# Three additions per state tile moved from Pool to DVE in the interleaved stage of a four-layer model

## The chip, the core and the metric

The kernel runs on one core of a Trainium2 chip. Its engines are PE (TensorE, matrix products), DVE (VectorE) and ACT (ScalarE), which work on tiles elementwise, Pool (GpSimd), which here rounds and splits weights and does some additions, and SP, which issues most of the transfers. The metric is the device time of one execution in microseconds, and the median of several executions is compared. PSUM, into which PE writes its products, is used here as eight banks of 128 x 512 fp32.

## The reference

Two models of two layers each follow one another on one sequence of 512 tokens and width 1024. The change touches only the second model, where each layer first mixes tokens in three ways, side by side: a state-space mixer, a gated spatial unit and a differential attention.

```python
def s5_mixer(u, a_re, a_im, log_dt, b_re, b_im, c_re, c_im, d_skip, w_glu, b_glu):
    ...
    bu = jnp.einsum("bsgh,gph->bsgp", uf.astype(jnp.complex64), b_bar)
    ...
    _, states = lax.associative_scan(combine, (a_seq, bu), axis=1)
    c_mat = lax.complex(c_re.astype(jnp.float32), c_im.astype(jnp.float32))
    y = jnp.real(jnp.einsum("bsgp,ghp->bsgh", states, c_mat))
    y = y + d_skip.astype(jnp.float32).reshape(SSM_GROUPS, SSM_GROUP) * uf
    y = jax.nn.gelu(y.reshape(bsz, seq, SSM_WIDTH))
    y = y * jax.nn.sigmoid(y @ w_glu.astype(jnp.float32) + b_glu.astype(jnp.float32))
    return y.astype(u.dtype)

def diff_attention(q, k, v, ...):
    ...
    def block(args):
        ...
        p = jax.nn.softmax(s, axis=-1)
        w = (p[:, :, 0] - lam * p[:, :, 1]).astype(v.dtype)
        return jnp.einsum("bhqk,bkhe->bqhe", w, v)
```

There are 16 groups of 64 complex states, that is 1024 states, or 8 tiles of 128 states by 512 positions. The rest of the reference (the first model, the projections and the feed-forward parts) is not touched.

## The kernel before

Every engine has its own program, written out by hand in the order in which it is to run; between them stand semaphores. There is no scheduler. A PSUM bank is named by a key such as ("yp", l, i). PE calls `claim(key)`: keys get the banks 0 to 7 in turn, and PE waits there until the key that had the bank eight claims earlier has been drained. `fill` reports that the bank is written, and the reader's `wait_filled` and `drain` answer to them.

The interleaved stage is run once for each of two layers (l = 0 and 1), from 1984 to 2080 us and from 2708 to 2804 us. It has 8 state tiles, i = 0 to 7, and 32 attention steps, most of them three to a state tile. For one state tile the work is:

- PE, `state_in(i)`: three products into three banks, keys ("bu", l, i, m) (L1123).
- DVE, `turn_in(i)`: three multiplications of these banks with tables of cosines and sums, which write turned[0], turned[1], turned[2] (L2256). This turns the complex input so that the recurrence becomes real.
- Pool: turned[1] = turned[0] + turned[1] and turned[2] = turned[0] - turned[2] (L1833, L1834).
- DVE, `scan(i)`: two scans along the 512 positions, which write z_re and z_im (L2266, L2268).
- Pool: z_sum = z_re + z_im (L1830).
- DVE, `turn_out(i)`: three multiplications that write out_parts (L2277, L2278, L2280).
- PE, `state_out(i)`: three products of out_parts, added up in one bank, key ("yp", l, i) (L1131).
- DVE, `add_y(l, i)`: adds that bank to yg and drains it (L2229 for i = 0 and 4, L2234 otherwise).

One attention step has scores on PE (L717), bias and row maximum on DVE (L1967), the exponential on ACT (L1340), a transposition on PE (L727), its copy on ACT (L1352), the product with v on PE (L739) and its scaling on DVE (L1984 or L1986, with L1976 and L1978 on two columns).

PE's order in tile i is `state_in(i + 1)`, `state_out(i - 1)`, then three attention steps. In tile 1 the gated spatial unit (L1113) stands between the first two. That makes 13 claims for a tile in the steady part, 3 + 1 + 9: ("yp", l, i - 1) is the fourth, and the claim eight places behind it is that of the transposition L727 in the third attention step of the same tile. So this transposition waits until `add_y(l, i - 1)` has drained its bank.

DVE's order in tile i is `scan(i)`, `turn_in(i + 1)`, one attention step, `turn_out(i)`, `add_y(l, i - 1)`, two attention steps. Pool does nothing else in this stage. z_re, z_im, z_sum and turned are single tiles in xnT, not doubled.

The lines of DVE's loop:

```python
scan(i)
if i < 7:
    turn_in(i + 1)
...
a0 = S5_STEPS * i - 3
attention(f"a2_{l}", a0, a0 + 1)
turn_out(i)
if i:
    add_y(l, i - 1)
attention(f"a2_{l}", a0 + 1, a0 + S5_STEPS)
```

Of the kernel before, what the change touches and what calls it, by code (L numbers as in the profile page):

```python
# [11 lines left out]
ALU = mybir.AluOpType  # L12
# [120 lines left out]
def build(nc, A, out, upto=99):  # L133
    ctx = ExitStack()
    with ctx:
# [123 lines left out]
        z_re, z_im, z_sum = (xnT[:, i, :] for i in range(3))  # L259
        turned = [xnT[:, 3 + i, :] for i in range(3)]  # L260
# [71 lines left out]
        def S(name):  # L332
            if name not in made:
                made[name] = ctx.enter_context(nc.semaphore(name))
            return made[name]
# [24 lines left out]
        def wait_filled(eng, key):  # L360
            eng.wait_ge(*filled_sem(key))
            return bank(key)
# [4 lines left out]
        def wait_drained(eng, key):  # L367
            eng.wait_ge(drained_sem(key), number[key] // BANKS + 1)
# [1231 lines left out]
        def _(pool):  # L1600
# [208 lines left out]
            for l in range(L2):  # L1809

                pool.dma_start(wn, A["gmlp_w_s_2"][l].rearrange("h i j -> i h j")).then_inc(S("gmlp_in"), 16)
                pool.dma_start(vgain, A["gmlp_v_g_2"][l:l + 1, :].broadcast_to([P, 256])).then_inc(S("gmlp_in"), 16)
                for i, name in enumerate(("lambda_q1_2", "lambda_k1_2", "lambda_q2_2", "lambda_k2_2")):
                    pool.dma_start(lamrow[:, i, :], A[name][l:l + 1, :].broadcast_to([P, 64])).then_inc(S("gmlp_in"), 16)
                pool.dma_start(subg, A["subln_g_2"][l:l + 1, :].broadcast_to([P, P])).then_inc(S("gmlp_in"), 16)
                pool.wait_ge(S("gmlp_in"), 16 * 7 * (l + 1))
                pool.memset(wn[0:64, :, 64:128], 0.0).then_inc(S("wn_ready"), 1)
                if l == 0:
                    wait_filled(pool, ("oh", NE - 1, 1))
                split(f"in{l}")  # L1820
                split(f"qk{l}", 2)
                rotary(groups2(l), f"g2_{l}", lambda i, l=l: split(f"qk{l}", 2))

                for i in range(-1, 8):
                    n = 8 * l + i
                    if i >= 0:
                        pool.wait_ge(S("scan_done"), n + 1)
                        if n:
                            pool.wait_ge(S("out_parts_ready"), n)
                        pool.tensor_tensor(z_sum, z_re, z_im, ALU.add).then_inc(S("z_sum_ready"), 1)  # L1830
                    if i < 7:
                        wait_drained(pool, ("bu", l, i + 1, 0))
                        pool.tensor_tensor(turned[1], turned[0], turned[1], ALU.add).then_inc(S("bu_turned"), 1)  # L1833
                        pool.tensor_tensor(turned[2], turned[0], turned[2], ALU.subtract).then_inc(S("bu_turned"), 1)  # L1834

                wait_filled(pool, ("mt", f"m2_{l}", NT - 1, 1))
                pool.wait_ge(S("y_copied"), 2 * (l + 1))
                split(f"out2_{l}")
                if upto <= 6 + 2 * l:
                    return  # L1840
                split(f"ff{l}")
                if upto <= 7 + 2 * l:
                    return
# [3 lines left out]
        def _(dve):  # L1847
# [107 lines left out]
            def attention(stage, first=-3, end=None):  # L1955
                base, todo = steps[stage]
                for i in range(first, len(todo) if end is None else end):
                    if i + 3 < len(todo):

                        u, t = todo[i + 3]  # L1960
                        j = base + i + 3
                        n = keys_of(u, t)
                        if i + 3 >= 3:
                            dve.wait_ge(S("probs_ready"), j - 2)
                        key = ("S", j)
                        ps = wait_filled(dve, key)
                        drain(dve.tensor_tensor_reduce(out=s_buf[:, j % 3, 0:n], in0=ps[:, 0:n], in1=bias_of(u, t),  # L1967
                                                       scale=1.0, scalar=3e38, op0=ALU.add, op1=ALU.min,
                                                       accum_out=nmx[:, j % 8:j % 8 + 1]), key)
                    if i >= 0:  # L1970
                        u, t = todo[i]
                        j = base + i
                        if i % 2 == 0:
                            dve.wait_ge(S("probs_ready"), j + 2)
                            pair_cf, gates = coef[:, j % 8:j % 8 + 2], gates_of(u, t)
                            link(dve.reciprocal(pair_cf, psumsum[:, j % 8:j % 8 + 2]))  # L1976
                            if gates is not None:
                                link(dve.tensor_tensor(pair_cf, pair_cf, gates, ALU.mult))  # L1978
                        cf = coef[:, j % 8:j % 8 + 1]
                        key = ("O", j)  # L1980
                        ps = wait_filled(dve, key)[:, u["at"]:u["at"] + u["w"]]
                        dst = u["dst"](t)
                        if u["first"]:
                            drain(dve.tensor_scalar(dst, ps, cf, None, ALU.mult), key)  # L1984
                        else:
                            drain(dve.scalar_tensor_tensor(out=dst, in0=ps, scalar=cf, in1=dst,  # L1986
                                                           op0=ALU.mult, op1=ALU.add), key)
# [248 lines left out]
            for l in range(L2):  # L2236
# [10 lines left out]
                def turn_in(i):  # L2247
# [5 lines left out]
                    for part, m, tab in ((0, 2, 0), (1, 1, 1), (2, 0, 2)):  # L2253
                        key = ("bu", l, i, m)
                        ps = wait_filled(dve, key)
                        drain(dve.tensor_tensor(turned[part], ps[:, :], tabs[:, tab, :], ALU.mult), key)  # L2256

                def scan(i):

                    n = 8 * l + i  # L2260
                    rb = s5("r")[:, n:n + 1].broadcast_to([P, T])
                    if n:
                        dve.wait_ge(S("out_parts_ready"), n)
                        dve.wait_ge(S("z_sum_ready"), n)
                    dve.wait_ge(S("bu_turned"), 2 * n + 1)
                    dve.tensor_tensor_scan(z_re, rb, turned[1], 0.0, ALU.mult, ALU.add)  # L2266
                    dve.wait_ge(S("bu_turned"), 2 * n + 2)
                    dve.tensor_tensor_scan(z_im, rb, turned[2], 0.0, ALU.mult, ALU.add).then_inc(S("scan_done"), 1)  # L2268

                def turn_out(i):  # L2270

                    n = 8 * l + i
                    tabs = s5_tabs[i % S5_BUFS]
                    dve.wait_ge(S("scan_done"), n + 1)
                    if i:
                        wait_filled(dve, ("yp", l, i - 1))
                    dve.tensor_tensor(out_parts[1], z_re, tabs[:, 1, :], ALU.mult)  # L2277
                    dve.tensor_tensor(out_parts[2], z_im, tabs[:, 2, :], ALU.mult)  # L2278
                    dve.wait_ge(S("z_sum_ready"), n + 1)
                    dve.tensor_tensor(out_parts[0], z_sum, tabs[:, 0, :], ALU.mult).then_inc(S("out_parts_ready"), 1)  # L2280
# [8 lines left out]
                for t in range(NT):  # L2289
                    dve.scalar_tensor_tensor(out=vn[:, t, :], in0=ugv[:, t, 256:512], scalar=s5("rstd")[:, t:t + 1],  # L2290
                                             in1=vgain, op0=ALU.mult, op1=ALU.mult).then_inc(S("vn_ready"), 1)
                for i in range(8):
                    scan(i)
                    if i < 7:
                        turn_in(i + 1)
                    if i == 1:
                        for t in range(NT):
                            ps = wait_filled(dve, ("sgu", l, t))
                            for h in range(4):
                                hs = slice(h * 64, (h + 1) * 64)  # L2300
                                ins = dve.scalar_tensor_tensor(out=ot2[:, t, hs], in0=ps[:, hs],
                                                               scalar=vcol("gmlp_b_s_2", 4 * l + h), in1=ugv[:, t, hs],
                                                               op0=ALU.add, op1=ALU.mult)
                            drain(ins, ("sgu", l, t))
                    a0 = S5_STEPS * i - 3
                    attention(f"a2_{l}", a0, a0 + 1)
                    turn_out(i)
                    if i:
                        add_y(l, i - 1)
                    attention(f"a2_{l}", a0 + 1, a0 + S5_STEPS)  # L2310
# [76 lines left out]
```

## Time and profile before

| | us |
|---|---|
| median of 3 runs | 3292.27 |
| lowest and highest | 3292.22, 3301.27 |
| the profiled execution | 3302.88 |
| its span, from first to last instruction | 3301.0 |
| what lies around the span | 1.9 |

The profiled execution is 10.6 us above the median and 1.6 us above the highest of the three runs. The page lists for each engine its busy time, and then groups of instructions. In the timelines a row gives the start, the time from that start to the end of the row's last instruction, the engine, the line, the operation with its tiles, and in brackets how long the engine had been idle and what ended the wait. Instructions of one engine overlap a little: the next one starts before the one ahead has fully ended, so what an instruction adds to a row of work is the distance between two starts.

### The profile page before, as it was taken

To read this page: it belongs to the slowest core of one execution; us is meant where nothing else is said; L and a number is where in the kernel's file an instruction comes from. 1 tells how busy PE (TensorE), PEld (TensorE's weight loads), DVE (VectorE), ACT (ScalarE), POOL (GpSimd) and SP (SyncE) were. 2 spreads that over 40 slices of the span, in tenths; PEclk is the share of its full clock that TensorE was granted. 3 is DMA by queue.
4 is the path that set the end of the run, shared out by engine and by line. 5 is a ranking of instruction groups with operands and counts; after the bars stand their busy time and mean duration, and the time that the engine had idled before them with its cause. 6 is when DMAs were issued, how large, how long until landed. Compare 5 with 4: busy or idle time off the path is not lost.

```text
span 3301.0 us, 38779 instructions
## 1 busy us (share of the span) xinstructions
PE 3084.8 (93%) x15349; PEld 2493.2 (76%) x15349; DVE 1052.6 (32%) x1975; ACT 718.9 (22%) x1608; POOL 1380.5 (42%) x1094
## 2 busy tenths in 40 slices
PE   6999988999899899999999898789999889689999
PEld 3546867888788899999999674478888765578887
DVE  1046632111243101111111218525243148335253
ACT  2136731001101111110110222422021222322020
POOL 0120045666465201007860253146666542256665
PEclk8999999999999899999999899799999999699999
DMA  6251012332332387777898413122333303122331
GB/s 177 79 153 25 3 52 79 94 102 83 82 97 77 105 227 200 198 193 217 236 269 218 133 33 114 48 75 88 91 98 96 86 29 127 39 77 87 100 98 48
DMA packets 535410, 365.71 MB, mean 111 GB/s; under 512 B 29980, under 2 KB 492023, under 8 KB 534712
## 3 DMA queue, kind: packets, MB, share of 16 engines
q1 hardware_dynamic: 523728, 327.85, 35.1%
q0 software_dynamic: 9088, 28.04, 2.9%
q10 hardware_dynamic: 2408, 7.27, 0.6%
q8 instruction: 126, 2.06, 0.3%
q14 instruction: 60, 0.49, 0.0%
HBM read 336.34 MB, written 26.77 MB: 110 GB/s over the span
## 4 chain that ended last, share of the span: by engine, by line
PE 88%; DVE 5%; ACT 3%; issue 3%; DMA 1%; ACTq 0%; POOL 0%; DVEq 0%; POOLq 0%
PE bank L574 16%; PE bank L575 16%; PE bank L576 16%; PE bank L649 15%; PE bank L1049 5%; PE bank L739 3%; PE bank L717 2%; PE bank L984 2%; DVE x_lo L1889 2%; PE bank L1019 2%; PE bank L727 2%; PE bank L1131 1%; PE bank L1123 1%; PE bank L692 1%; ACT arena L1271 1%
## 5 line engine op out<-in xcount | busy, mean ns | idle before, releaser
L1618 POOL TENSOR_SCALAR unit_parts<-ring 128x1024 fp32r<-128x1024 f32 (+1 forms) x296 | 309.9, 1047 | 984.4 <-PE bank L576 669.6
L1620 POOL TENSOR_TENSOR unit_parts<-ring,unit_parts 128x1024 fp32r<-128x1024 f32 (+1 forms) x296 | 708.4, 2393 | 24.7
L574 PE MATMUL bank<-x_hi,unit_parts 128*128 128x512 f32 x1408 | 570.4, 405 | 44.8 <-DVE x_lo L1889 44.8
L575 PE MATMUL bank<-x_lo,unit_parts 128*128 128x512 f32 x1408 | 565.3, 401 | 0.0
L576 PE MATMUL bank<-x_hi,unit_parts 128*128 128x512 f32 x1408 | 556.5, 395 | 0.0
L649 PE MATMUL bank<-arena,ring 128*128 128x160 f32 x2816 | 385.1, 299 | 0.0
L649 PEld LDWEIGHTS bank<-arena,ring 128*128 128x128 f32 x2816 | 383.0, 190 | 0.3 <-ACT arena L1473 0.2
L574 PEld LDWEIGHTS bank<-x_hi,unit_parts 128*128 128x128 f32 x1408 | 266.9, 190 | 120.0 <-DVE x_lo L1889 47.2
L576 PEld LDWEIGHTS bank<-x_hi,unit_parts 128*128 128x128 f32 x1408 | 267.3, 190 | 67.2
L575 PEld LDWEIGHTS bank<-x_lo,unit_parts 128*128 128x128 f32 x1408 | 267.6, 190 | 63.4 <-issue 2.9
L576 PE MATMUL bank<-unit_parts,hid_parts 128*128 128x512 f32 x592 | 230.4, 389 | 0.0
L575 PE MATMUL bank<-unit_parts,hid_parts 128*128 128x512 f32 x592 | 230.4, 389 | 0.0
L574 PE MATMUL bank<-unit_parts,hid_parts 128*128 128x512 f32 x592 | 230.3, 389 | 0.0
L1712 POOL TENSOR_TENSOR arena<-arena 128x1024 f32<-128x1024 f32 (+9 forms) x48 | 69.8, 1455 | 356.4 <-ACT arena L1495 355.8
L1997 DVE TENSOR_TENSOR x<-bank,x 128x512 f32<-128x512 f32 x80 | 55.4, 692 | 435.6 <-PE bank L576 435.6
L1049 PE MATMUL bank<-arena,ring 128*128 128x160 f32 x1408 | 192.8, 299 | 0.5 <-DMA ring<-in_moe_w_down 0.5
L1049 PEld LDWEIGHTS bank<-arena,ring 128*128 128x128 f32 x1408 | 191.6, 190 | 0.9 <-DMA ring<-in_moe_w_down 0.7
L2349 DVE TENSOR_TENSOR whole<-arena 128x512 f32<-128x512 f32 x44 | 117.0, 2659 | 220.6 <-ACT arena L1590 220.5
L1584 ACT ACTIVATE arena<-bank,vec 128x512 f32<-128x512 f32 x88 | 68.5, 779 | 496.5 <-PE bank L576 496.5
L1425 ACT ACTIVATE arena<-bank 128x160 f32<-128x160 f32 (+1 forms) x110 | 40.0, 364 | 591.2 <-PE bank L649 315.9
L574 PE MATMUL bank<-unit_parts,x_hi 128*128 128x512 f32 x320 | 128.9, 403 | 34.9 <-DVE x_lo L1889 34.9
L1932 DVE SCALAR_TENSOR_TENSOR arena<-bank,vec,arena 128x512 f32<-128x512 f32 (+2 forms) x42 | 30.9, 737 | 382.5 <-ACT arena L1326 240.0
(269 smaller groups left out, 4254.8 us busy)
## 6 DMA issues: line engine op xcount, KB each, us to landing
ring<-in_moe_w_gate SPq DMA_DIRECT2D x88, 512.0 KB, 5.9
ring<-in_moe_w_up SPq DMA_DIRECT2D x88, 512.0 KB, 6.8
ring<-in_moe_w_down SPq DMA_DIRECT2D x64, 704.0 KB, 4.6
ring<-in_w_up SPq DMA_DIRECT2D x88, 512.0 KB, 5.1
ring<-in_w_down SPq DMA_DIRECT2D x16, 1024.0 KB, 5.0
ring<-in_od_w_in SPq DMA_DIRECT2D x24, 512.0 KB, 5.1
s_stream<-arena POOLq DMA_DIRECT2D x12, 1024.0 KB, 9.2
arena<-s_stream SPq DMA_DIRECT2D x16, 768.0 KB, 4.3
```

Source lines behind the costliest of these rows:

```text
L574: pe.matmul(ps, a[0], b[0], start=start, stop=False)
L575: pe.matmul(ps, a[0], b[1], start=False, stop=False)
L576: return pe.matmul(ps, a[1], b[0], start=False, stop=stop)
L649: ins = pe.matmul(ps[rows_at:rows_at + m, 0:n], w[:, k * width + at:k * width + at + m], src[:, k, :], start=k == 0, stop=k == KD - 1)
L717: ins = pe.matmul(ps[:, 0:k.shape[1]], u["q"](t), k, start=k is ks[0], stop=k is ks[-1])
L739: ins = pe.matmul(ps[:, 0:u["vw"]], pT_buf[0:w, j % 2, kt * P:kt * P + P], u["v"](kt, w), start=kt == 0, stop=kt == kts - 1)
L1049: ins = pe.matmul(ps[:, (m - m0) * CAP:(m - m0 + 1) * CAP], w[:, k * P:(k + 1) * P], hidE[:, k, :], start=k == 0, stop=k == KE - 1)
L1584: act.activation(acc[:, 2 * a + n % 2, :], ps[:, :], ACT.Identity, scale=vcol("conv_w_2", 132 * l + 88 + f), bias=vcol("conv_b_2", 44 * l ...
L1618: pool.tensor_scalar(hi, raw, 1.0, 1.0, ALU.mult, ALU.mult).then_inc(S("units_rounded"), 1)
L1620: pool.tensor_tensor(lo, raw, hi.bitcast(F32), ALU.subtract).then_inc(S("units_split"), 1)
L1712: tt = lambda o, a, b, op: link(pool.tensor_tensor(o, a, b, op))
L2349: dve.tensor_tensor(next_whole(hid_hi[:, j % KE, :], hid_lo[:, j % KE, :]), gg[:, n % 2, :], acc[:, 2 + n % 2, :], ALU.mult).then_inc(S("g ...
```

## The change

Pool's loop over the state tiles is taken out. DVE gets a new function, `turn_in_sums(i)`, with the two additions that follow `turn_in(i)`. It is called ahead of `scan(0)` for i = 0, and for the others in tile i between the first attention step and `turn_out(i)`. The third addition, z_sum, becomes the first operation in `turn_out`. The wait on z_sum_ready ahead of the scans goes away. Tiles, buffers, and the orders of PE and ACT stay as they are.

```diff
--- before.py
+++ after.py
@@ -1821,18 +1821,6 @@
-                for i in range(-1, 8):
-                    n = 8 * l + i
-                    if i >= 0:
-                        pool.wait_ge(S("scan_done"), n + 1)
-                        if n:
-                            pool.wait_ge(S("out_parts_ready"), n)
-                        pool.tensor_tensor(z_sum, z_re, z_im, ALU.add).then_inc(S("z_sum_ready"), 1)
-                    if i < 7:
-                        wait_drained(pool, ("bu", l, i + 1, 0))
-                        pool.tensor_tensor(turned[1], turned[0], turned[1], ALU.add).then_inc(S("bu_turned"), 1)
-                        pool.tensor_tensor(turned[2], turned[0], turned[2], ALU.subtract).then_inc(S("bu_turned"), 1)
@@ -2255,13 +2243,18 @@
+                def turn_in_sums(i):
+
+                    wait_drained(dve, ("bu", l, i, 0))
+                    dve.tensor_tensor(turned[1], turned[0], turned[1], ALU.add).then_inc(S("bu_turned"), 1)
+                    dve.tensor_tensor(turned[2], turned[0], turned[2], ALU.subtract).then_inc(S("bu_turned"), 1)
+
                 def scan(i):
...
                     if n:
                         dve.wait_ge(S("out_parts_ready"), n)
-                        dve.wait_ge(S("z_sum_ready"), n)
@@ -2274,6 +2267,7 @@
                     if i:
                         wait_filled(dve, ("yp", l, i - 1))
+                    dve.tensor_tensor(z_sum, z_re, z_im, ALU.add).then_inc(S("z_sum_ready"), 1)
                     dve.tensor_tensor(out_parts[1], z_re, tabs[:, 1, :], ALU.mult)
@@ -2289,6 +2283,7 @@
+                turn_in_sums(0)
                 for i in range(8):
                     scan(i)
@@ -2304,6 +2299,8 @@
                     attention(f"a2_{l}", a0, a0 + 1)
+                    if i < 7:
+                        turn_in_sums(i + 1)
                     turn_out(i)
                     if i:
                         add_y(l, i - 1)
```

DVE in tile 2 of layer 0, from the first attention step (L1967, L1984) to `add_y` (L2234) and the attention behind it; small is a tile of single columns:

```order
L1967 ISA arena,small<-bank,cst 128x384
L1967 ISA small 128x1
L1984 TENSOR_SCALAR arena<-bank,small 128x128
L2277 TENSOR_TENSOR xnT<-xnT,arena 128x512
L2278 TENSOR_TENSOR arena<-xnT,arena 128x512
L2280 TENSOR_TENSOR xnT<-xnT,arena 128x512
L2234 TENSOR_TENSOR arena<-arena,bank 128x512
```

The same place in the changed kernel (L2249 and L2250 are the two sums of the next tile, L2270 is z_sum, and L2222 is `add_y`):

```order
L1955 ISA arena,small<-bank,cst 128x384
L1955 ISA small 128x1
L1972 TENSOR_SCALAR arena<-bank,small 128x128
L2249 TENSOR_TENSOR xnT<-xnT 128x512
L2250 TENSOR_TENSOR xnT<-xnT 128x512
L2270 TENSOR_TENSOR xnT<-xnT 128x512
L2271 TENSOR_TENSOR xnT<-xnT,arena 128x512
L2272 TENSOR_TENSOR arena<-xnT,arena 128x512
L2274 TENSOR_TENSOR xnT<-xnT,arena 128x512
L2222 TENSOR_TENSOR arena<-arena,bank 128x512
```

Three rows have come in between the attention step and `add_y`, all ahead of it.

DVE at the start of the stage in layer 0, from `turn_in(0)` (L2256) over small work and four operations for the spatial unit (L2290) to `scan(0)` (L2266, L2268):

```order
L2256 TENSOR_TENSOR xnT<-bank,arena 128x512 x3
L2066 TENSOR_TENSOR small<-small 128x1
L2066 TENSOR_TENSOR small<-small,cst 128x1
L2286 TENSOR_SCALAR small<-small 128x1
L2290 SCALAR_TENSOR_TENSOR arena<-arena,s5small,cst 128x256 x4
L2266 SCALAR_TENSOR_TENSOR xnT<-s5small,xnT 128x512
L2268 SCALAR_TENSOR_TENSOR xnT<-s5small,xnT 128x512
```

The same place in the changed kernel:

```order
L2244 TENSOR_TENSOR xnT<-bank,arena 128x512 x3
L2054 TENSOR_TENSOR small<-small 128x1
L2054 TENSOR_TENSOR small<-small,cst 128x1
L2280 TENSOR_SCALAR small<-small 128x1
L2284 SCALAR_TENSOR_TENSOR arena<-arena,s5small,cst 128x256 x4
L2249 TENSOR_TENSOR xnT<-xnT 128x512
L2250 TENSOR_TENSOR xnT<-xnT 128x512
L2259 SCALAR_TENSOR_TENSOR xnT<-s5small,xnT 128x512
```

The two sums of tile 0 stand directly ahead of the first scan.

## Rows read from the trace of the kernel before

**Rows 1.** Page, busy time of each engine: us, share of span, instructions.

```profile
PE 3084.8 (93%) x15349; PEld 2493.2 (76%) x15349; DVE 1052.6 (32%) x1975; ACT 718.9 (22%) x1608; POOL 1380.5 (42%) x1094
```

**Rows 2.** Busy time by stretch: the steady part of the stage in either layer.

```profile
2010.00:2078.00 68.00, 62.47 (x250) 34.01 (x251) 57.26 (x128) 19.09 (x59) 20.08 (x16) 1.00 0.40 144
2734.00:2802.00 68.00, 62.46 (x250) 33.92 (x249) 57.22 (x129) 19.26 (x58) 20.10 (x16) 1.00 0.40 143
```

**Rows 3.** Groups by line, 1984 to 2082 us: Pool; busy, mean ns, idle before.

```profile
L1830 POOL TENSOR_TENSOR xnT<-xnT 128x512 f32<-128x512 f32 x8 | 10.2, 1270 | 51.4 <-DVE xnT L2268 51.4
```

**Rows 4.** Waits, 1984 to 2080 us: waiting line, releasing line, us, times, longest.

```profile
DVE arena L1967 <- PE bank L717: 8.1, 7, 1.8
```

**Rows 5.** Timeline of DVE, tile 2 of layer 0; the last row is tile 7.

```profile
2019.26 0.56 DVE L1967 CUSTOM_DVE_ANT_0 arena<-bank,cst 128x384 f32<-128x384 f32 x1 [1.51 <-PE bank L717]
...
2020.58 0.68 DVE L2277 TENSOR_TENSOR xnT<-xnT,arena 128x512 f32<-128x512 f32 x1
...
2022.38 0.68 DVE L2234 TENSOR_TENSOR arena<-arena,bank 128x512 f32<-128x512 f32 x1
...
2075.71 0.68 DVE L2234 TENSOR_TENSOR arena<-arena,bank 128x512 f32<-128x512 f32 x1
```

**Rows 6.** Timeline of PE: the third step's transposition, tiles 1 to 7, layer 0.

```profile
2011.80 0.66 PE L727 MATMUL bank<-cst,arena 128*128 128x128 f32 x4 [1.27 <-DVE arena L2229]
...
2023.12 0.55 PE L727 MATMUL bank<-cst,arena 128*128 128x128 f32 x3 [0.78 <-DVE arena L2234]
...
2034.39 0.44 PE L727 MATMUL bank<-cst,arena 128*128 128x128 f32 x2 [0.20 <-DVE arena L2234]
...
2045.30 0.33 PE L727 MATMUL bank<-cst,arena 128*128 128x128 f32 x1 [1.03 <-DVE arena L2234]
...
2056.76 0.66 PE L727 MATMUL bank<-cst,arena 128*128 128x128 f32 x4 [1.46 <-DVE arena L2229]
...
2068.07 0.55 PE L727 MATMUL bank<-cst,arena 128*128 128x128 f32 x3 [0.79 <-DVE arena L2234]
...
2076.50 0.44 PE L727 MATMUL bank<-cst,arena 128*128 128x128 f32 x2
```

**Rows 7.** Timeline of DVE: operations that ran beside Pool's, layer 0.

```profile
1986.62 1.25 DVE L2066 TENSOR_TENSOR small<-small,cst 128x1 f32<-128x1 f32 x1
1987.90 0.15 DVE L2286 TENSOR_SCALAR small<-small 128x1 f32<-128x1 f32 x1
1988.09 2.45 DVE L2290 SCALAR_TENSOR_TENSOR arena<-arena,s5small,cst 128x256 f32<-128x256 f32 x4
...
1994.84 1.77 DVE L2277 TENSOR_TENSOR xnT<-xnT,arena 128x512 f32<-128x512 f32 x1
...
2030.58 0.97 DVE L1978 TENSOR_TENSOR small<-small 128x2 f32<-128x2 f32 x1
...
2041.85 1.59 DVE L2277 TENSOR_TENSOR xnT<-xnT,arena 128x512 f32<-128x512 f32 x1
```

**Rows 8.** Timeline of PE: gaps elsewhere, and state_in at either clock.

```profile
120.23 1.10 PE L838 MATMUL bank<-ring,xnT 128*128 128x256 f32 x4 [2.44 <-DVE arena L1932]
...
200.35 0.63 PE L895 MATMUL bank<-ring,small 128*31 128x64 f32 x8 [2.50 <-DVE arena L1932]
...
1995.83 4.94 PE L1123 MATMUL bank<-arena 128*128 128x512 f32 x6
...
2012.96 2.74 PE L1123 MATMUL bank<-arena,cst 128*128 128x512 f32 x6
...
2088.40 0.63 PE L727 MATMUL bank<-cst,arena 128*128 128x128 f32 x4 [2.37 <-ACT arena L1340]
```

**Rows 9.** Busy time by stretch; the granted clock is third from last.

```profile
122.00:126.00 4.00, 4.00 (x28) 3.72 (x28) 0.00 (x0) 1.93 (x4) 1.29 (x3) 1.00 0.43 131
...
201.00:205.00 4.00, 4.00 (x7) 1.72 (x8) 0.00 (x0) 1.03 (x3) 0.00 (x0) 0.57 1.05 385
...
2089.00:2112.00 23.00, 23.00 (x75) 15.62 (x74) 6.70 (x26) 7.60 (x23) 0.00 (x0) 0.50 0.07 16
```

## The prediction

> **What bounds the kernel now.** PE is busy for 93% of the span, DVE for 32% and Pool for 42% [rows 1]. That average does not settle this case, since the change touches only two stretches of about 96 us. In the steady part of each, over 68 us, PE is busy for 62.5 us and DVE for 57.3 us [rows 2]: two nearly full engines which also wait for each other. The two layers agree within 0.1 us, so I work out layer 0 and double it.
>
> Pool is the first thing to look at. Its additions take 1.27 us each, and ahead of z_sum alone it idles for 51.4 us until DVE lets it go [rows 3]. The other direction is missing: DVE idles in this stretch for 8.1 us ahead of L1967, until PE has written scores [rows 4], and nowhere for Pool. So Pool's latency is hidden today, and taking it away gains nothing by itself.
>
> Next comes the loop between PE and DVE. In tile 2 DVE gets its scores at 2019.26 after 1.51 us of idleness, and then runs without a gap to `add_y` at 2022.38 [rows 5], apart from about half a microsecond in the attention step. PE meanwhile waits at the transposition of the third attention step, in this tile for 0.78 us, until `add_y` has drained the bank [rows 6]. The same wait stands in all of tiles 1 to 6: 1.27, 0.78, 0.20, 1.03, 1.46 and 0.79 us. Behind it PE has a few small products, `state_in`, `state_out` and the next scores, for which DVE waits. So one turn of the loop is a PE part, from `add_y` to the scores, and a DVE part, from the scores to `add_y`, one behind the other. What is added to the DVE part lengthens the turn by all of it. DVE's idle time lies on the other side of the loop, ahead of the scores, and cannot take it up.
>
> **The additions on DVE.** They are not in the trace on DVE, but three operations of the same kind and size are: L2277, L2278 and L2280 fill the time from 2020.58 to 2022.38, thus 0.60 us each, and one lasts 0.68 us from start to end [rows 5]. The cost is between 0.60 us, if they overlap as these do, and 0.68 us, if not. Neither of the sums reads what the operation ahead of it wrote, so I take 0.60: three cost 1.80 us a tile (up to 2.04).
>
> - Tiles 1 to 6: the two sums and z_sum all stand between the scores and `add_y`. That is 6 x 1.80 = +10.8 us.
> - Tile 7: it has no next sums, and PE did not wait for `add_y` at its transposition at 2076.50 [rows 6]. Only z_sum is added, 0.6 us, and PE's slack is about 0.1 us there, since `add_y` starts at 2075.71 and ends 0.68 later [rows 5]: +0.5.
> - Start of the stage: DVE is alone on the path from `turn_in(0)` to the first scores. The two sums add 1.20 us. But L2066 takes 1.25 us there on 128 x 1 elements, where its neighbour L2286 takes 0.15, and the four L2290 span 2.45 us, some 0.63 us over an even step of 0.42; both run while Pool adds [rows 7]. Without Pool 1.10 + 0.63 = 1.73 us go away: -0.5 in sum.
> - Tile 0, behind the first scores: PE goes through `state_in`, the spatial unit and `state_out` before it gives the next scores, so 1.8 us more on DVE are covered. The cover is DVE's wait ahead of the scores at tile 1, one of those of rows 4, and besides L2277 and its successor, which take 1.77 us here [rows 7] and would fall to 0.68, give 2.1 us back.
>
> **The end of Pool's company.** Two further operations in the DVE part of the loop are stretched while Pool works: L1978 in tile 3 takes 0.97 us on two columns and L2277 in tile 4 takes 1.59 [rows 7], against 0.15 (taking L2286 as the measure of such small ones) and 0.68 [rows 5, 7]. They give back 0.8 + 0.9 = 1.7 us. The Trainium skill (GPSIMD Engine Reference, Key points) says that Pool shares its SBUF interfaces with DVE and contends with DVE instructions that have two SBUF inputs; by that rule the trace agrees, since the stretched ones are of that kind.
>
> In sum a layer gets 10.8 + 0.5 - 0.5 - 1.7 = +9.1 us, and two layers get +18.2.
>
> **The clock.** What comes on top is in PE's gaps. With 1.80 us more, less what the end of the company gives back, the gaps of tiles 1 to 6 become 3.07, 2.58, 1.20, 1.93, 3.26 and 2.59 us. Today's longest in this stretch, 1.46 us, leaves the granted clock at 1.00, that is 2.4 GHz [rows 2]. Longer ones exist elsewhere. After 2.37 us of idleness the clock is 0.50 (1.2 GHz) from 2089 on, and after 2.50 us it is 0.57 on average over 201 to 205, thus half for some 3.4 of the 4 us; a gap of 2.44 us at 120.23 has no such effect [rows 8, 9]. In the whole trace I find ten gaps of 2.1 to 3.5 us that begin at full clock, three of which are those rows; eight have half clock within 2.5 us of their end. Four gaps of a layer fall in this class, eight in all: 8 x 0.8 = 6.4 falls. The six matmuls of `state_in` take 4.94 us at 1995.83, behind a gap of 7 us, and 2.74 us at 2012.96 [rows 8], so 3.4 us at half lose 3.4 x (1 - 2.74/4.94) = 1.5 us. Dense products follow each gap, as after 200.35, so one such spell is the nearest case; a second spell makes it 3.0. I take 2.0 us a fall: 6.4 x 2.0 = +12.8 us, with bounds of 0 (no fall) and 10 x 3.0 = 30 (all eight, the two of 1.93 us too, twice as long).
>
> **Rivals.** *Serial work alone.* The clock stays full because each gap is short beside the dense work around it; for this speak the gap at 120.23 and its like. Then +18.2 us remain. *Covered.* The wait of PE is put down to `add_y`, but if something else of that time held it, the additions could fill DVE's 8.1 us of idleness a layer [rows 4] and cost little: 8 x 1.80 = 14.4, less 8.1, less the 5.5 (1.73 + 2.1 + 1.7) that the end of Pool's company gives, is +0.8 a layer, +1.6 in all. Against it speaks the place: DVE idles before the scores, and the sums stand behind them. *Faster by the end of the company.* If on top of that PE did not wait for `add_y` at all, only the gains of rows 7 would count, 1.73 + 1.7 = 3.4 us a layer or -6.9 us. It decides as soon as PE's slack at the transposition is above 1.8 us; rows 6 show a wait in six of eight tiles, so no slack. *DVE is the better engine anyway.* Two sums take 2 x 1.27 = 2.54 us on Pool [rows 3] and would take 1.20 on DVE; were scans released by them, 16 x 1.34 = 21 us would be gained. Against it: no scan waits for Pool today. The Trainium skill (GPSIMD Engine Reference, Key points) holds that DVE is about twice as fast for elementwise work. By that rule the trace agrees on the durations, 1.27 against 0.68 us, and leaves the conclusion out, since nothing waits for the sums. *It does not do what it says*: the additions do not overlap with their neighbours and cost 0.68 us each, 2.04 instead of 1.80 a tile; that is +2.9 us over 12 tiles and lies in the range.
>
> **How the numbers follow.** The profiled execution took 3302.88 us. With falls of the clock it becomes 3302.88 + 18.2 + 12.8 = 3333.9; set on the median of the runs, which is 10.6 lower, 3292.27 + 31.0 = 3323.3. This has a chance of 0.57. Serial work alone gives 3292.27 + 18.2 = 3310.5, chance 0.29. Covered gives 3293.9, chance 0.09; faster by the end of the company gives 3285.4, chance 0.03; DVE as the better engine gives 3271, chance 0.02. A measurement of this kernel tells some 0.3% from no change, here 9.9 us. The first two are slower by more: 0.86. Covered and most of the company case lie within: 0.11. Faster: 0.03. The range goes from 3305, a serial cost somewhat below its sum, to 3345, all falls at nearly their upper bound or the likeliest case upon the highest of the three runs.
>
> **What would show it.** In the changed profile the three additions should take 0.68 us each on DVE, 48 in all, at steps of 0.60. PE's idle time ahead of the third step's transposition should have grown to the six figures above; if it grew less, the loop is not what I read. L2277 and its successor should show no case of over 0.7 us. DVE's idle time ahead of the scores should be as before, or larger where the clock fell. The granted clock over the two steady stretches should be below 1.00; at 1.00 the term of 12.8 us is wrong. If the stretches lengthen by under 5 us each, the loop is wrong too.

## The result, and the profile after

| | before | after |
|---|---|---|
| median of 6 runs, us | 3293.29 | 3322.31 |
| lowest to highest | 3292.22 to 3301.27 | 3319.99 to 3325.37 |
| profiled execution / its span | 3302.88 / 3301.0 | 3323.03 / 3321.2 |

The changed kernel is slower by a ratio of 1.0081, 95% interval 1.0068 to 1.0094. That is 29.0 us by the medians and 20.2 us by the two profiles. The forecast was 3323.3 us in a range of 3305 to 3345.

The same place as [rows 5], the timeline of DVE in tile 2 of layer 0, now reads (L1955 are the scores, L2222 is `add_y`):

```profile
2025.08 0.56 DVE L1955 CUSTOM_DVE_ANT_0 arena<-bank,cst 128x384 f32<-128x384 f32 x1 [1.57 <-PE bank L717]
...
2026.39 0.68 DVE L2249 TENSOR_TENSOR xnT<-xnT 128x512 f32<-128x512 f32 x1
2026.99 0.68 DVE L2250 TENSOR_TENSOR xnT<-xnT 128x512 f32<-128x512 f32 x1
2027.59 0.68 DVE L2270 TENSOR_TENSOR xnT<-xnT 128x512 f32<-128x512 f32 x1
2028.19 0.68 DVE L2271 TENSOR_TENSOR xnT<-xnT,arena 128x512 f32<-128x512 f32 x1
...
2030.00 0.68 DVE L2222 TENSOR_TENSOR arena<-arena,bank 128x512 f32<-128x512 f32 x1
```

The three additions take 0.60 us from start to start and 0.68 from start to end. From the scores to `add_y` DVE needs 4.92 us, where it needed 3.12. DVE's wait ahead of the scores is still there, 1.57 us against 1.51: it took up nothing.

The timeline of PE at the third step's transposition in tiles 1 to 7 of layer 0 answers [rows 6]:

```profile
2015.94 0.66 PE L727 MATMUL bank<-cst,arena 128*128 128x128 f32 x4 [3.08 <-DVE arena L2217]
...
2030.73 0.91 PE L727 MATMUL bank<-cst,arena 128*128 128x128 f32 x3 [2.59 <-DVE arena L2222]
...
2044.89 0.44 PE L727 MATMUL bank<-cst,arena 128*128 128x128 f32 x2 [1.68 <-DVE arena L2222]
...
2056.69 0.33 PE L727 MATMUL bank<-cst,arena 128*128 128x128 f32 x1 [1.93 <-DVE arena L2222]
...
2071.64 1.12 PE L727 MATMUL bank<-cst,arena 128*128 128x128 f32 x4 [3.27 <-DVE arena L2217]
...
2086.18 0.90 PE L727 MATMUL bank<-cst,arena 128*128 128x128 f32 x3 [2.59 <-DVE arena L2222]
...
2097.84 0.44 PE L727 MATMUL bank<-cst,arena 128*128 128x128 f32 x2 [0.48 <-DVE arena L2222]
```

The forecast had said 3.07, 2.58, 1.20, 1.93, 3.26 and 2.59 us; only the third is off. The transpositions at 2030.73 and 2086.18 also last 0.9 us, where that of tile 2 took 0.55 in [rows 6]: the clock. By stretch (PE, PE weight load, DVE, ACT and Pool busy; then the granted clock, the DMA share and GB/s) the steady part and what lies behind it read:

```profile
2010.00:2091.00 81.00, 65.87 (x230) 36.68 (x230) 63.53 (x136) 18.17 (x54) 0.00 (x0) 0.88 0.36 129
2016.70:2020.00 3.30, 3.30 (x9) 1.88 (x8) 2.18 (x4) 1.07 (x3) 0.00 (x0) 0.50 0.01 2
...
2034.00:2057.00 23.00, 19.40 (x77) 10.33 (x77) 19.36 (x42) 4.51 (x13) 0.00 (x0) 1.00 0.30 103
...
2103.00:2126.00 23.00, 19.56 (x100) 12.50 (x100) 8.30 (x33) 13.98 (x33) 0.00 (x0) 1.00 0.17 46
```

The steady part has a mean clock of 0.88 where it had 1.00 [rows 2]. At 0.50 or 1.00 that is 81 x 0.12 / 0.5 = 19.4 us at half. Between the gaps of tiles 2 and 4, with only the 1.68 us of tile 3 there, it stays at 1.00. The last line is a surprise. The 23 us from the first product of the gated linear unit (GLU) on are at full clock now; before, half clock ruled most of the same work, from 2089 on [rows 9].

The ends of the stretches are starts in PE's timeline: the stage goes from the first matmul of `state_in(0)` (L1123) to the first of the GLU (L1154), the tail from there to the first transposition of the mixed rows (L750). In layer 0 after the change:

```profile
1984.50 1.88 PE L1123 MATMUL bank<-arena,cst 128*128 128x512 f32 x4
...
2103.03 3.70 PE L1154 MATMUL bank<-arena,ring 128*128 128x512 f32 x8 [0.62 <-ACT arena L1548]
...
2135.82 1.54 PE L750 MATMUL bank<-cst,arena 128*128 128x128 f32 x6 [10.45 <-DVE arena L2318]
```

| profile | stage, layer 0 / 1 | tail, layer 0 / 1 | median | before, beside it |
|---|---|---|---|---|
| before | 99.9 / 99.8 | 42.8 / 42.8 | 3293.3 | |
| after | 118.5 / 118.3 | 32.8 / 32.8 | 3322.3 | 3293.3 |
| e1, sums only | 112.2 / 111.9 | 32.8 / 41.6 | 3316.3 | 3298.3 |
| e2, z_sum only | 108.7 / 108.9 | 32.8 / 41.6 | 3308.7 | 3298.3 |
| e3, behind turn_in | 100.0 / 101.5 | 42.8 / 32.8 | 3298.8 | 3298.3 |
| e4, gaps filled, too long | 114.7 / 114.7 | 42.8 / 32.8 | 3324.4 | 3298.3 |
| e4b, gaps filled | 109.7 / 109.6 | 42.8 / 42.8 | 3323.2 | 3299.1 |
| e5, before, tail filled | 99.9 / 99.9 | 32.8 / 32.8 | 3284.3 | 3299.1 |
| e6, before, add_y first | 96.5 / 96.3 | 42.8 / 42.9 | 3296.4 | 3299.1 |
| e7, after, add_y first | 98.8 / 98.7 | 41.6 / 41.6 | 3300.1 | 3299.1 |
| e11, after again | 118.5 / 121.5 | 32.8 / 32.8 | 3320.4 (one) | 3297.2 |
| e12, after, tail filled | 118.5 / 121.4 | 32.8 / 32.8 | 3322.4 | 3297.2 |
| e9, behind, first, tail | 97.7 / 97.6 | 32.8 / 32.8 | 3279.7 | 3297.2 |
| e10, first, tail, on Pool | 96.4 / 96.3 | 32.8 / 32.8 | 3272.9 | 3297.2 |

Between the two profiles both stages grow by 18.7 and 18.5 us, 37.2 in sum, and both tails shrink by 10.0, 20.0 in sum. That leaves 17.2 of the 20.2 us; the other 3.0 lie outside these stretches, 2.7 of them already ahead of the first stage (1984.50 against 1981.85), where nothing was changed.

### The profile page after: what moved, and what is told of

It is laid out like the page before. It is cut to its first block, busy times and chain, and to the rows that moved or that the text cites. A ratio compares the mean times of both kernels' runs of the same rounds, so it can differ in the third digit from the quotient of the medians.

```text
span 3321.2 us, 38764 instructions
## 1 busy us (share of the span) xinstructions
PE 3084.4 (93%) x15349; PEld 2491.4 (75%) x15349; DVE 1071.7 (32%) x2023; ACT 718.5 (22%) x1608; POOL 1317.3 (40%) x1046
## 4 chain that ended last, share of the span: by engine, by line
PE 87%; DVE 6%; ACT 3%; issue 3%; DMA 0%; ACTq 0%; POOL 0%; DVEq 0%; POOLq 0%
PE bank L574 16%; PE bank L575 16%; PE bank L576 16%; PE bank L649 15%; PE bank L1049 5%; PE bank L739 3%; PE bank L984 2%; DVE x_lo L1877 2%; PE bank L717 2%; PE bank L1019 2%; PE bank L727 2%; PE bank L1123 1%; PE bank L1131 1%; PE bank L692 1%; ACT arena L1271 1%
```

## The experiments

My theory had three parts: additions between the scores and `add_y` are paid in full; the gaps they make in PE's work bring the clock down; the whole is a matter of place. The first rival was load: DVE is nearly full, and 1.8 us more a tile cost what they cost wherever they stand.

**e1 and e2, one part of the change alone.** The additions that stay on Pool run there in their old loop.

The edit of the changed kernel for e1, and then that for e2:

```diff
+                for i in range(8):
+                    n = 8 * l + i
+                    pool.wait_ge(S("scan_done"), n + 1)
+                    if n:
+                        pool.wait_ge(S("out_parts_ready"), n)
+                    pool.tensor_tensor(z_sum, z_re, z_im, ALU.add).then_inc(S("z_sum_ready"), 1)
...
-                    dve.tensor_tensor(z_sum, z_re, z_im, ALU.add).then_inc(S("z_sum_ready"), 1)
```

```diff
+                for i in range(8):
+                    wait_drained(pool, ("bu", l, i, 0))
+                    pool.tensor_tensor(turned[1], turned[0], turned[1], ALU.add).then_inc(S("bu_turned"), 1)
+                    pool.tensor_tensor(turned[2], turned[0], turned[2], ALU.subtract).then_inc(S("bu_turned"), 1)
...
-                turn_in_sums(0)
...
-                    if i < 7:
-                        turn_in_sums(i + 1)
```

> DVE does only the two sums, Pool keeps z_sum. A layer's stage is read here from the first state_in matmul to the first matmul behind the last attention tile's GLU (L1154 in the kernel before): 99.8 us before, 118.6 and 118.3 after the whole change. Loop theory: 6 x 1.20 us of serial work, less 1.7 and 0.5 for the end of the sums on Pool, is +5.0 us a layer, and PE's gaps ahead of the third transposition become 2.5, 2.0, 0.6, 1.3, 2.7 and 2.0 us; the two to four of 2 us and more bring a fall of the clock each at 1.5 to 2 us, so +8 to +13 us a layer over 99.8 and +16 to +26 in the whole. If the clock played no part: +5 a layer, +10 in the whole. If DVE's load as such were the cause and not the place, the stage grows by two thirds of 18.6, +12.4 a layer, whatever the gaps are.

> DVE does only z_sum, inside turn_out; Pool keeps the two sums. Loop theory: 6 x 0.60 + 0.5 = +4.1 us a layer, nothing given back, since it is the sums on Pool that stretch DVE's operations. PE's gaps become 1.9, 1.4, 0.8, 1.6, 2.1 and 1.4 us, so at most two falls of the clock: a stage of 104 to 107 us, +8 to +15 us in the whole. Without the clock +8.2 in the whole. By load alone a third of 18.6: +6.2 a layer, 106 us.

The sums alone gave a stage of 112.2 and 111.9 us and a ratio of 1.006 (1.0041 to 1.0079); z_sum alone 108.7 and 108.9 us and 1.0037 (1.0024 to 1.0049). The loop theory gave 108 to 113 for e1, which holds it, and 104 to 107 for e2, which lies 1.8 us above. The gaps of e1, again of the third transposition:

```profile
2012.09 0.66 PE L727 MATMUL bank<-cst,arena 128*128 128x128 f32 x4 [2.47 <-DVE arena L2224]
...
2026.30 0.55 PE L727 MATMUL bank<-cst,arena 128*128 128x128 f32 x3 [1.99 <-DVE arena L2229]
...
2040.14 0.44 PE L727 MATMUL bank<-cst,arena 128*128 128x128 f32 x2 [1.07 <-DVE arena L2229]
```

2.5 and 2.0 us came as expected, the third is again 0.5 us too long. In e2 three falls of the clock a layer stand in the stage and not two: one or two of these follow gaps of 1.39 us. Both whole times lie within their forecasts (+18.0 us in +16 to +26, +10.4 in +8 to +15). By load alone e1 should have had 112.2 us, which it met, and e2 106, which it did not. These two runs do not tell place from load; the next one does.

**e3, the same additions in another place.** All three stand on DVE directly behind `turn_in`, where DVE waits for the scores.

```diff
-                    dve.tensor_tensor(z_sum, z_re, z_im, ALU.add).then_inc(S("z_sum_ready"), 1)
...
                     if i < 7:
                         turn_in(i + 1)
+                    dve.wait_ge(S("scan_done"), 8 * l + i + 1)
+                    dve.tensor_tensor(z_sum, z_re, z_im, ALU.add).then_inc(S("z_sum_ready"), 1)
+                    if i < 7:
+                        turn_in_sums(i + 1)
...
-                    if i < 7:
-                        turn_in_sums(i + 1)
                     turn_out(i)
```

> The same three additions on DVE, but directly behind turn_in, where DVE waits for PE's scores, and not between the scores and add_y. Loop theory: only what exceeds DVE's waits there counts (0.6, 0.3, 0.7, 1.35, 0 and 0.3 us in tiles 1 to 6), less 1.7 and 0.5 given back: +1.1 us a layer, stage 101 us, PE's gaps as in the kernel before or smaller, granted clock 1.00 in the steady part, the whole within 3 us of the kernel before. If DVE's load were the cause and not the place, the stage is 118 us as after the change.

The stage is 100.0 and 101.5 us, the ratio 1.0000 (0.9985 to 1.0015). So it is the place: the same work on the same engine is 18.5 us cheaper in layer 0 and 16.8 in layer 1. The forecast of a full clock in the steady part held in layer 0 only; in layer 1 one fall followed a gap of 1.46 us. DVE's timeline in tile 2 shows where it went:

```profile
2022.02 0.68 DVE L2291 TENSOR_TENSOR xnT<-xnT 128x512 f32<-128x512 f32 x1
2022.62 0.68 DVE L2249 TENSOR_TENSOR xnT<-xnT 128x512 f32<-128x512 f32 x1
2023.22 0.69 DVE L2250 TENSOR_TENSOR xnT<-xnT 128x512 f32<-128x512 f32 x1
2023.82 0.55 DVE L1955 CUSTOM_DVE_ANT_0 arena<-bank,cst 128x384 f32<-128x384 f32 x1
```

The scores follow without a wait. I had left one thing out: in tile 0 the additions now stand ahead of the first scores, and PE's first gap there is 8.07 us against 6.93 before. The steady part made up for it, in full in layer 0.

**e4 and e4b, the clock apart from the rest.** Matmuls whose result is thrown away fill PE's gaps in the changed kernel. They write into the bank that the scores of the third step then overwrite.

```diff
                         ps = claim(("S", base + i + 3))
+                        if stage in ("a2_0", "a2_1") and i + 3 in FILL:
+                            for _ in range(FILL[i + 3]):
+                                pe.matmul(ps[:, :], c("ident"), qD[:, 0, :], start=True, stop=True)
```

> The changed kernel with four more matmuls of 128 x 512 (0.43 us each, thrown away: the bank's own scores follow with start set) ahead of the scores of the third attention step in tiles 1, 2, 4, 5 and 6. They lie in PE's gap and nobody waits for them. Clock theory: the gaps fall to 0.2 to 1.5 us, the granted clock stays at 1.00 from tile 1 on, and the stage loses its falls: 118.5 - 9.3 = 109 us, which is the serial part alone (+9.1 a layer), the whole 3304 to 3312. If the falls are no consequence of the gaps, or cost nothing: 118 us, 3320 or more.

The stage was 114.7 us, neither 109 nor 118. My fill was mis-sized: four matmuls took 3.60 us, not 1.7, since one of them is two rows of the trace (x8 in the timeline's row). They outlasted every gap but the one I had left alone in tile 3, so PE's own extra work lengthened the stage and e4 says nothing on the clock's price.

```profile
2012.94 3.60 PE L716 MATMUL bank<-arena,cst 128*128 128x512 f32 x8
```

> The changed kernel with thrown-away matmuls in PE's gaps again, now with their true length: one of 128 x 512 takes two rows of 0.43 us, so four of them were 3.4 us, longer than the gaps of the run before. Here 2, 2, 1, 2, 3 and 2 of them in tiles 1 to 6 (1.7, 1.7, 0.9, 1.7, 2.6 and 1.7 us), each shorter than its gap of 3.08, 2.59, 1.68, 1.93, 3.27 and 2.59. Clock theory: the gaps left are under 1.5 us, no fall of the clock in the stage, which keeps the serial part alone: 99.8 + 9.1 = 108.9 us (109.4 with the gap of tile 3 as measured). If the falls cost nothing or don't hang on the gaps: 118.5 us.

With fills shorter than the gaps the stage is 109.7 and 109.6 us. The granted clock of e4b over the steady part is 1.00:

```profile
2012.00:2090.00 78.00, 72.69 (x277) 37.77 (x276) 66.80 (x145) 18.90 (x58) 0.00 (x0) 1.00 0.36 129
```

This is the cleanest reading of the two terms. The serial part is 109.65 - 99.8 = +9.8 us a layer, and the clock is 118.4 - 109.65 = +8.8 us. Only PE's idleness was changed between the two kernels, so the gaps do bring the clock down. Yet the whole kernel was not clearly faster for it: 3323.2 us against 3322.3, or 24.1 us above the kernel before beside it, where the change had 29.0 above its own. The table says why: in the profile of e4b both tails are back at 42.8 us, which gives back the 17.5 us gained in the stages.

**e5, e11 and e12, the tail.** Behind the GLU PE idles for 2.37 us [rows 8], and in some executions half clock follows for over 20 us. Two thrown-away matmuls stand in this gap, written into the bank of the transposition that waits there.

```diff
                         ps = claim(("T", j))
+                        if stage in ("a2_0", "a2_1") and i == 8 * S5_STEPS - 2:
+                            for _ in range(2):
+                                pe.matmul(ps[:, :], c("ident"), qD[:, 0, :], start=True, stop=True)
                         pe.wait_ge(S("probs_ready"), j + 1)
```

> The kernel before with two thrown-away matmuls (1.7 us) behind the GLU products, in the gap of 2.37 us ahead of a transposition, written into the bank that this transposition overwrites. Theory: this gap is what starts, in some executions and not in others, the half clock of 20 to 24 us in the last attention steps; with the gap at 0.6 us it starts in none. The stretch from the GLU's first matmul to the transposition of the mixed rows is then 32.8 us in both layers (42.8 twice in the profile before, 32.8 twice after the change), the stage stays at 99.8, and the whole is 3280 to 3285 us, with less spread than before. Rival: the long half clock is a matter of the low load of these steps itself; then 42.8 us stands in one or both layers and the whole stays at 3298.

The kernel before with this edit has tails of 32.8 us in both layers, a median of 3284.3 us (3281.4 to 3286.6) and a ratio of 0.9941 (0.9922 to 0.9959). Its gap is nearly closed:

```profile
2085.43 1.98 PE L726 MATMUL bank<-arena,cst 128*128 128x512 f32 x4
2087.78 0.66 PE L730 MATMUL bank<-cst,arena 128*128 128x128 f32 x4 [0.36 <-ACT arena L1343]
```

So without this gap there is no long spell: with it filled none of eight tails is long (e5, e12, e9 and e10). Without the edit the kernel before ranged from 3286.6 to 3309.8 us beside it, over 23 us in 19 runs, where e5 ranged over 5 in 4.

> The changed kernel once more, for its clock behind the stage. In its first profile the stretch from the GLU to the transposition of the mixed rows took 32.8 us in both layers, without the long half clock. If the change takes that spell away regularly (its own falls of the clock shift what comes behind), both layers stand at 32.8 again; if it was luck, 41 to 43 us in at least one of them. The stage is 118.5 either way.

> The changed kernel with the two thrown-away matmuls (1.7 us) behind the GLU products that took the late half clock from the kernel before. If the changed kernel had no such spell in its timed runs, nothing is gained: 3320 to 3323 us, stage 118.5, stretch behind it 32.8. If its timed runs had one on average, 3310 us.

The changed kernel once more had tails of 32.8 us in both layers, and with the tail filled it gained nothing: 3322.4 us. So the changed kernel did not have the spell in any of the four tails profiled, although its gap of 2.37 us is still there, and its timed runs speak for the same. In its profile the kernel before paid 20 us there.

The other half of e11's forecast, a stage of 118.5 us "either way", failed in layer 1: 121.5 us, and 121.4 in e12. There the gap of 1.68 us in tile 3 was followed by half clock, which it was not in the first profile, and the fall of tile 2 lasted twice as long. From PE's timeline and by stretch (columns as above):

```profile
2774.58 0.44 PE L727 MATMUL bank<-cst,arena 128*128 128x128 f32 x2 [1.68 <-DVE arena L2222]
...
2775.20:2778.50 3.30, 3.30 (x6) 1.24 (x5) 3.26 (x7) 1.52 (x5) 0.00 (x0) 0.50 0.00 0
```

So the clock term of the same kernel differs by 3 us a layer from one execution to the next.

What does the gap of the tail need besides its length? The profiles with this gap left open fall into two classes. Where the stage had no fall of the clock behind its start (before, e4b, e6, e7, and layer 0 of e3), nine of nine tails are long. Where it had falls (after, e11, e1, e2, e4, and layer 1 of e3), three of eleven are. That goes together with the falls in the stage, but no run shows that they are the cause. A rival stands untested: the falls also shift the moment at which the gap comes, and the moment may be what counts. That the length of a gap alone does not decide is seen in tile 3 of the changed kernel, where the same gap of 1.68 us brought a fall in layer 1 of e11 and of e12 and none in the other four stages.

**e6 and e7, add_y first.** The wait that carries the whole argument is tried directly: `add_y` drains its bank before DVE turns the states back.

In e6 the lines are those of the kernel before, in e7 those of the changed kernel, where the sums stand between the two places:

```diff
                     attention(f"a2_{l}", a0, a0 + 1)
+                    if i:
+                        add_y(l, i - 1)
...
                     turn_out(i)
-                    if i:
-                        add_y(l, i - 1)
```

> The kernel before, additions on Pool, with add_y ahead of turn_out in DVE's order. Loop theory: PE's wait at the third transposition is for add_y's bank, so draining it 1.8 us sooner removes the gaps of 1.27, 0.78, 0.20, 1.03, 1.46 and 0.79 us: 5.5 us a layer, stage 94.3 us, or up to 96 where the next wait stands close behind; -8 to -11 us in the whole. Rival: something else of that time holds PE (probabilities from ACT): stage unchanged at 99.8.

> The changed kernel, additions on DVE, with add_y directly behind the first attention step, ahead of the sums and turn_out. Loop theory: PE is let go before the additions are done, so they leave the loop; PE's gaps at the third transposition go to 0, no falls of the clock but that of the start, and DVE becomes nearly full (about 11.2 us of work in a turn): stage 98 to 101 us instead of 118.5, the whole within 5 us of the kernel before. Rival, load: 1.8 us more on DVE a tile cost what they cost wherever they stand: stage 112 us or more.

In e6, with the additions on Pool, the stage fell from 99.8 to 96.5 and 96.3 us. PE's waits in the steady part no longer name DVE, but the tables of the next state tile:

```profile
PE bank L727 <- ACT arena L1340: 6.9, 1, 6.9
PE bank L1123 <- DMA arena<-s_stream: 0.9, 2, 0.5
PE bank L1123 <- DMA cst<-s_stream: 0.5, 1, 0.5
```

That confirms the wait and shows the next one behind it. The forecast of 94.3 to 96 us was missed by 0.3 to 0.5, and that of the whole by more: -8 to -11 us were forecast, and the median is 2.7 us lower, 3296.4 us, ratio 0.9987 (0.9968 to 1.0006), which can't be told from no change. The two stages gained 6.8 us in the profile; both of its tails are long, as they were before. In e7, with the additions on DVE, the stage is 98.8 and 98.7 us instead of 118.5, and the ratio 1.0004 (0.9988 to 1.0021). DVE and PE are then both nearly full (64.1 and 64.3 of 67 us):

```profile
2010.00:2077.00 67.00, 64.32 (x248) 33.79 (x246) 64.06 (x147) 20.89 (x60) 0.00 (x0) 1.00 0.39 138
```

The load of 1.8 us a tile costs 2.3 us a layer here (e7 against e6), and 18.7 in the place that the change gave it.

**e9 and e10, the best of both.** Both take e5's fill and `add_y` ahead of `turn_out`. e10 leaves the additions on Pool; e9 has them on DVE behind `turn_in`, as e3.

Their edits are those shown above, put together; the part that both share is:

```diff
+                        if stage in ("a2_0", "a2_1") and i == 8 * S5_STEPS - 2:
+                            for _ in range(2):
+                                pe.matmul(ps[:, :], c("ident"), qD[:, 0, :], start=True, stop=True)
...
                     attention(f"a2_{l}", a0, a0 + 1)
+                    if i:
+                        add_y(l, i - 1)
                     turn_out(i)
-                    if i:
-                        add_y(l, i - 1)
```

> The kernel before with add_y ahead of turn_out and with the two thrown-away matmuls behind the GLU products, the two edits that each made the stage or the stretch behind it shorter. They act in different stretches and should add up: stage 96.4 and stretch behind it 32.8 us in both layers; 3284 - 2 x 3.4 = 3277 us.

> All three additions on DVE, directly behind turn_in, add_y ahead of turn_out, and the two thrown-away matmuls behind the GLU products: the change placed as the loop theory wants it. DVE is nearly full, so the stage is about that of the run with add_y first (98.7 us) or 1 us less, the stretch behind it 32.8: 3282 us, some 5 us above the same edits with the additions on Pool. If DVE's waits for the scores take up the additions wholly: 96.4 and 3277 us.

e10 took 3272.9 us (3271.2 to 3276.7), ratio 0.9929 (0.9910 to 0.9948); e9 took 3279.7 us, ratio 0.9948 (0.9929 to 0.9967). Both are faster than the kernel before and the changed one. The stages and tails add up as expected; the whole of e10 is 4 us below its forecast of 3277, that of e9 2 us below 3282. The additions are still better on Pool, by 1.3 us a layer in the stage. The medians differ by 6.8 us; 3.6 us of difference stand ahead of the first stage in the two profiles, where the kernels are the same.

## Why the prediction came out right, point by point

**The loop between PE and DVE** was read rightly. e6 removed PE's gaps by moving `add_y` alone, and e3 and e7 made the additions cheap (0.2 and 1.8 us a layer in e3, 2.3 in e7) by taking them out from between scores and `add_y`.

**The serial term** was +9.1 us a layer and measured +9.8 (e4b). Most of the difference is tile 3. I had let the stretched L1978 give back 0.8 us, but DVE then only waited for the product behind it:

```profile
2039.59 0.16 DVE L1966 TENSOR_TENSOR small<-small 128x2 f32<-128x2 f32 x1
2040.27 0.35 DVE L1974 SCALAR_TENSOR_TENSOR arena<-bank,small,arena 128x128 f32<-128x128 f32 x1 [0.52 <-PE bank L739]
```

The stretched operation had covered a wait of 0.5 us; the gap became 1.68 us and not 1.20.

**The end of Pool's company** came as expected at the start of the stage, where [rows 7] had 1.25 and 2.45 us. PE's first gap there shrank from 6.93 to 6.26 us, 0.7 for the 0.5 of the forecast:

```profile
1989.26 0.16 DVE L2054 TENSOR_TENSOR small<-small,cst 128x1 f32<-128x1 f32 x1
...
1989.64 1.67 DVE L2284 SCALAR_TENSOR_TENSOR arena<-arena,s5small,cst 128x256 f32<-128x256 f32 x4
```

Nor are the operations of `turn_out` stretched any more; by line (busy, mean ns, idle before) their means over the stage are

```profile
L2272 DVE TENSOR_TENSOR arena<-xnT,arena 128x512 f32<-128x512 f32 x8 | 5.5, 685 | 0.0
L2271 DVE TENSOR_TENSOR xnT<-xnT,arena 128x512 f32<-128x512 f32 x8 | 5.5, 685 | 0.0
```

e2, where Pool kept the sums, had the first gap of the stage at 6.9 us as before, and e1, where Pool kept only z_sum, at 6.3 as after: it is the two sums that had stretched DVE. By the Trainium skill (GPSIMD Engine Reference, Key points) it is DVE instructions with two SBUF inputs that contend with Pool. The trace agrees: the stretched ones were of that kind, and `turn_in`, with one input from PSUM, stayed at 0.68 to 0.69 us beside Pool too.

**The clock term** was mis-sized: 6.4 falls at 2.0 us, +12.8 in the kernel, against 8.8 a layer, +17.6. The price of half clock was right: 8.8 us for 19.4 us at half is 0.45 us for each, and 1.5 for 3.4 is 0.44. Each fall came to 1.8 us (17.6 for ten), near the 2.0 of the forecast. The count was low. I had let one gap in five go without a fall and had left out the two of 1.93 us, except in the upper bound; in the first profile falls followed the gaps of tiles 1, 2, 4, 5 and 6 in both layers, with that of tile 6 twice as long as the others, and only the one of 1.68 us in tile 3 had none. In e11 and e12 it had one in layer 1.

**The tail** was missing from the working altogether, and it is what made the sum right. Stages: forecast +31.0, measured +37.2. Tails: forecast 0, measured -20.0 between the profiles. Against the medians, with 29.0 us, the tails and all else give back 8.2 us. That fits timed runs of the kernel before which did not all have two long spells: of the 19 beside e5 the five fastest (to 3290.2 us) have a mean clock of 0.963 to 0.967, the five slowest (from 3303.9 us) 0.956 to 0.959. No profile shows such a run, so the share of the tails in them stays an inference. The forecast of 3323.3 against 3322.3 owes its closeness to luck, to two errors of opposite sign: 6.2 us too few in the stages, and nothing for the tails. The size of the base was uncertain too: beside the later experiments the kernel before had medians of 3297 to 3299 us, against which the change costs 25 us (e12's neighbours), and 29 against its own.

**The rivals.** "Serial work alone" is refuted by the clock of 0.88 and by e4b. "Covered" is what e3 shows for another place, not for this one: +0.5 us (with about 5 us either way by its interval), against the +1.6 it was priced at. "DVE is the better engine" did not come; Pool's latency was hidden, and e10 beats e9 with Pool.

## What to carry to other kernels

Before moving work between engines, find the loop that two engines turn in, and see on which side of the wait the new instructions stand: three additions a tile cost 18.5 to 18.7 us a layer between the scores and the drained bank, and 0.2 to 1.8 us one attention step earlier. Look then at the gaps which a serial cost opens on TensorE; here 9.8 us of serial work a layer brought another 8.8 by the clock. And measure the stretches one by one, since a clock spell elsewhere can take or give back as much as the whole edit.

## What the runs showed of the hardware

- In the stage of the changed kernel every gap of PE of 1.9 to 3.3 us brought the granted clock to 0.50, ten of ten in its first profile, and the two of 1.68 us did not. That is no sharp bound: gaps of 1.68 us were followed by a fall in both layers of e4 and in layer 1 of e11 and e12, one of 1.46 us was in e3, and three of four of 1.39 us in e2, while in e2 one of 1.86 us, in e7 both of 1.79 us and in the changed kernel's tails all four of 2.37 us were not.
- Matmuls whose result is overwritten keep the clock up: 8.8 us a layer in e4b, and 10.0 in each tail of e5 against the long ones.
- After the 2.37 us gap of the tail, attention steps that kept PE busy for 23.00 of 23 us at half clock [rows 9] did not bring the full clock back. In the fourteen profiles the clock was at half for 20.5 to 23.9 us on end in each of the twelve long tails. The same steps keep the full clock when they begin at it, and the tail is then 10.0 us shorter. Why they don't release it, and why profiles with falls in their stage mostly lack this spell, stays open.
- An operation that another engine stretches can hide a wait behind it, so its excess is an upper bound of what its end gives back: 0.8 us of stretch gave 0.3 in tile 3.
